# Latent attention: rotary partner by shifted products on VectorE, two banks for the first projections, and a part of the output projection in the last steps

## The reference

```python
def _mla(x, w_in, g_q, g_kv, w_uq, w_uk, w_uv, w_o, pos):
    h = x @ w_in                                   # 1024 -> 384 + 256 + 64
    c_q = _rmsnorm(h[..., :384], g_q)
    c_kv = _rmsnorm(h[..., 384:640], g_kv)
    k_r = _rope(h[..., 640:], pos)                 # one 64-wide rotary key for all heads
    q = einsum('bsr,rhd->bshd', c_q, w_uq)         # 8 heads of 128 + 64
    q_n, q_r = q[..., :128], _rope(q[..., 128:], pos)
    # scores: q_n . (w_uk c_kv) + q_r . k_r, scaled, causal; softmax; values w_uv c_kv
    return o @ w_o                                 # 1024 -> 1024
def _rope(x, pos):                                 # half = 32
    x1, x2 = x[..., :half], x[..., half:]
    return concatenate([x1 * cos - x2 * sin, x1 * sin + x2 * cos], -1)
```

## Time and profile before

| | |
|---|---|
| median of 3 runs | 2545.45 us (2542.76 to 2547.97) |
| the profiled execution's own time | 2543.65 us |
| its span | 2541.9 us |
| busy: PE, DVE, ACT, POOL | 2452.6, 1114.9, 886.0, 114.6 us |
| mean granted TensorE clock | 0.99 |
| matmuls | 11784 |

### The profile page before, as it was taken

The page is one execution under the profiler, slowest core; times in us unless marked ns, Lnnn a source line. Parts: engine busy times, 40 slices in busy tenths (PEclk is TensorE's granted clock), DMA queues, the critical chain, the costliest instruction groups (busy, mean ns, idle before and its releaser), DMA issues.

```text
span 2541.9 us, 29499 instructions
## 1 busy us (share of the span) xinstructions
PE 2452.6 (96%) x11784; PEld 2024.5 (80%) x11784; DVE 1114.9 (44%) x1487; ACT 886.0 (35%) x1444; POOL 114.6 (5%) x169
## 2 busy tenths in 40 slices
PE   7798999999989999998999999999999999999997
PEld 7577888888878788887888888888877788888886
DVE  3355633445665543346455322223245524433334
ACT  3232422323443332235444323332245534522222
POOL 3000200000100100000000000000000000000001
PEclk9999999999999999999999999999999999999999
DMA  5512332222311323322222222222321122322221
GB/s 161 75 54 67 117 100 100 90 92 83 108 42 50 118 98 100 99 100 67 78 71 81 92 92 83 83 83 84 104 67 50 51 94 80 108 99 91 96 94 67
DMA packets 187063, 220.32 MB, mean 87 GB/s; under 512 B 20531, under 2 KB 141568, under 8 KB 186832
## 3 DMA queue, kind: packets, MB, share of 16 engines
q1 hardware_dynamic: 183200, 206.13, 25.4%
q0 software_dynamic: 3760, 12.73, 2.4%
HBM read 213.60 MB, written 5.24 MB: 86 GB/s over the span
## 4 chain that ended last, share of the span: by engine, by line
PE 89%; DVE 6%; ACT 3%; issue 1%; DMA 1%; POOL 0%; SPq 0%; ACTq 0%; POOLq 0%; DVEq 0%
PE A L507 46%; PE B L507 40%; DVE WL L1754 2%; PE C L507 1%; ACT WH L1186 1%; DMA X<-in_x 1%; DVE Y L1912 1%; PE C L876 0%; PE C L1091 0%; DVE YL L1969 0%; DVE st L1893 0%; PE C L932 0%; ACT ar L1262 0%; DVE ar L1967 0%; ACT XH L1189 0%
## 5 line engine op out<-in xcount | busy, mean ns | idle before, releaser
L1754 DVE TENSOR_TENSOR WL<-RAW,WH 128x2048 fp32r<-128x2048 f32 (+1 forms) x197 | 448.8, 2278 | 690.1 <-ACT WH L1186 690.1
L1186 ACT ACTIVATE WH<-RAW 128x2048 fp32r<-128x2048 f32 (+1 forms) x197 | 370.9, 1883 | 626.0 <-PE A L507 561.1
L507 PE MATMUL B<-XH,WH 128*128 128x512 f32 (+1 forms) x1440 | 548.2, 385 | 8.7 <-DVE WL L1754 5.4
L507 PE MATMUL B<-XH,WL 128*128 128x512 f32 (+1 forms) x1440 | 539.9, 379 | 0.0
L507 PE MATMUL B<-XL,WH 128*128 128x512 f32 (+1 forms) x1440 | 526.5, 381 | 6.4 <-DVE XL L1769 6.3
L507 PE MATMUL A<-WH,YH 128*128 128x512 f32 x944 | 367.7, 390 | 1.6 <-DVE YL L2243 1.6
L507 PE MATMUL A<-WH,YL 128*128 128x512 f32 x944 | 367.3, 389 | 0.0
L507 PE MATMUL A<-WL,YH 128*128 128x512 f32 x944 | 367.2, 389 | 0.0
L507 PEld LDWEIGHTS B<-XH,WH 128*128 128x128 f32 x1440 | 271.8, 189 | 78.2 <-issue 16.4
L507 PEld LDWEIGHTS B<-XH,WL 128*128 128x128 f32 x1440 | 272.0, 189 | 51.3
L507 PEld LDWEIGHTS B<-XL,WH 128*128 128x128 f32 x1440 | 263.7, 190 | 57.1 <-DVE XL L1769 8.3
(11 more groups left out here) (290 smaller groups left out, 2125.9 us busy)
## 6 DMA issues: line engine op xcount, KB each, us to landing
RAW<-in_w_in SPq DMA_DIRECT2D x33, 1024.0 KB, 5.1
RAW<-in_mlp_w_up SPq DMA_DIRECT2D x32, 1024.0 KB, 5.2
RAW<-in_mlp_w_down SPq DMA_DIRECT2D x32, 1024.0 KB, 5.0
RAW<-in_w_in SPq DMA_DIRECT2D x48, 512.0 KB, 4.3
RAW<-in_w_ffn_in SPq DMA_DIRECT2D x22, 1024.0 KB, 5.1
RAW<-in_w_ffn_out SPq DMA_DIRECT2D x10, 1024.0 KB, 5.0
RAW<-in_mla_w_o SPq DMA_DIRECT2D x4, 1024.0 KB, 5.1
RAW<-in_swa_w_q SPq DMA_DIRECT2D x4, 1024.0 KB, 4.9
```

What stands on the lines that cost most here:

```text
L507: return nc.tensor.matmul(dst, l, r, start=first, stop=last)
L1186: nc.scalar.activation(WH[s][:, 0:n], RAW[s][:, 0:n], ACT.Copy).then_inc(hi_ready, 1)
L1754: tt(WL[s][:, 0:n], RAW[s][:, 0:n], f32(WH[s][:, 0:n]), ALU.subtract).then_inc(lo_ready, 1)
```

## The change

It makes these edits. Rotary partner: the second version of the rotary key and unit 5 of every pair are gone, with their loads; VectorE makes the sine product by four multiplications of 32 rows each, which read the bank 32 rows away (`rotated`). A pair has seven units now (0, 1 queries, 2 rotary queries, 3, 4 keys, 5, 6 values), its chunk 1664 columns. Stage "in": the rope matmuls of each half stand ahead of that half's keys, the queries are transposed between the halves, and the keys after two units of pair 0. The first eleven units alternate between B[0] and B[1]. The splits of chunks 8 and 10 come earlier in steps 1 and 5. Four groups of the output projection (first chunk, first 512 columns) run in steps 11 to 14 in B[0], and VectorE adds them to alpha x. GpSimd's constants wait for x, its first two gain vectors come after the roots, and its bias additions wait for one more chunk of the MLP. The split of chunk "if + 1", the low halves of the third norm, and the whole end of the feed-forward have new places: its last half runs block by block, gains are multiplied ahead of the root, ScalarE makes the root, and stores go by halves.

```diff
-    ("in", 4, 2, 2, 7, 1, 0),
+    ("in", 4, 2, 0, 7, 1, 0),
+    def unit_bank(n):
+        return n % 2 if n < PAIR_AHEAD else 0
+    def unit_taken(n):
+        if n < PAIR_AHEAD:
+            return s_("pair_u%d" % (n % 2)), n // 2 + 1
+        return s_("pair_u0"), (PAIR_AHEAD + 1) // 2 + n - PAIR_AHEAD + 1
+    def units_of(j):
+        i = (j + 6) // T
+        return i, () if i >= PAIRS else ((4,), (5, 6), (0, 1), (2, 3))[j % T]
-    PAIRS, PAIR_STEPS, PAIR_UNITS = 4, 16, 8
+    PAIRS, PAIR_STEPS, PAIR_UNITS, PAIR_AHEAD = 4, 16, 7, 11
@@ SP, end
+            for h in range(2):
+                cols = slice(512 * h, 512 * h + 512)
+                sp.wait_ge(s_("fin_x"), 2 * t + h + 1)
+                sp.dma_start(out[0, tok(t), cols], X[:, t, cols]).then_inc(s_("stored"), 16)
@@ TensorE
+        in_rope(0)
...
+        in_keys(0)
+        in_rope(1).then_inc(s_("in_rope"), 1)
+        queries_by_feature()
+        in_keys(1)
...
+            if n >= PAIR_AHEAD:
+                pe.wait_ge(*unit_taken(n - 1))
+            elif n >= 2:
+                pe.wait_ge(*unit_taken(n - 2))
+            elif n == 1:
+                pe.wait_ge(s_("rope_taken"), 1)
...
+        def output_part(t):
+            if t == 0:
+                pe.wait_ge(lo_ready, c + 1)
+                pe.wait_ge(*unit_taken(PAIRS * PAIR_UNITS - 1))
+                pe.wait_ge(s_("pair_lo"), 8)
+            else:
+                pe.wait_ge(s_("wo_x"), t)
+            for k in range(4):
+                r = mm3(B[0][:], XH[:, k, tok(t)], XL[:, k, tok(t)], wh[:, k, :], wl[:, k, :], k == 0, k == 3)
+        pair_unit(0, 0)
+        pair_unit(0, 1)
+        keys_by_feature()
+        for u in range(2, PAIR_UNITS):
             pair_unit(0, u)
...
-            i, u = (j + 6) // T, 2 * ((j + 2) % T)
-            if i < PAIRS:
-                pair_unit(i, u)
+            i, us = units_of(j)
+            for u in us[:1]:
+                pair_unit(i, u)
+            if 10 < j < 15:
+                output_part(j - 11)
             pair_values(j)
-            if i < PAIRS:
-                pair_unit(i, u + 1)
+            for u in us[1:]:
+                pair_unit(i, u)
...
-        tokens_half(BASE["wo0"][0], 0, BASE["wo0"][1], XH, XL)
+        tokens(BASE["wo0"][0] + 1, slot(BASE["wo0"][0] + 1), XH, XL, 4, 4, 512, BASE["wo0"][1])
...
+        for t, kh in ((0, 0), (1, 0), (0, 1), (1, 1), (2, 0), (2, 1), (3, 0), (3, 1)):
+            nk = (4, 2)[kh]
@@ ScalarE
+            if j in (1, 5):
+                split(c0 + 4 + j // 2, more=16 * 2 + 192 + 64 * (j // T))
             if j + 2 < PAIR_STEPS:
                 pair_exp(j + 2)
...
+        split(BASE["if"][0] + 1)
         then_root("pre", 3)
...
+                if h:
+                    act.wait_ge(s_("fin_ss"), T + t + 1)
+                    act.wait_ge(s_("fin_half"), t + 1)
+                    nc.scalar.activation(stat(RS + t), stat(SS + 4 + t), ACT.Sqrt, bias=stat(SS + t)).then_inc(s_("fin_root"), 1)
@@ VectorE
+        def rotated(bank, scale=None):
+            half = ROPE // 2
+            for q in range(4):
+                to, of = slice(half * q, half * q + half), slice(half * (q ^ 1), half * (q ^ 1) + half)
+                if scale:
+                    x = stt(M_T[to, 1, :], bank[of, :], scale, sinT[to, :], ALU.mult, ALU.mult)
+                else:
+                    x = tt(M_T[to, 1, :], bank[of, :], sinT[to, :], ALU.mult)
+            return x
...
+                then(rotated(bank))
+                x = tt(M_T[:, 0, :], bank[:], cosT, ALU.mult)
...
+            x = X[:, t, 0:512]
+            stt(x, x, ALPHA, B[0][:], ALU.mult, ALU.add).then_inc(s_("wo_x"), 1)
...
+            if t == 3:
+                lo_half("post", 0, range(4), NG2, ALU.mult)
             product_out(1, t)
...
+        def first_half(t):
+            dve.wait_ge(s_("fin_ss"), t + 1)
+            then(tt(Y[:, t, 0:512], Y[:, t, 0:512], GB[:, 0, 0:512], ALU.mult))
+            ts(stat(SS + t), stat(SS + t), RMS_EPS, None, ALU.add).then_inc(s_("fin_half"), 1)
+        def add_normed(t):
+            dve.wait_ge(a_free[t], ra + 6)
+            then(tt(xtmp[:, t % 2, :], Y[:, t, 512:1024], GB[:, 0, 512:1024], ALU.mult))
+            dve.wait_ge(s_("fin_root"), t + 1)
+            then(nc.vector.reciprocal(stat(RS + t), stat(RS + t)))
+            for h, y in enumerate((Y[:, t, 0:512], xtmp[:, t % 2, :])):
+                x = X[:, t, 512 * h:512 * h + 512]
+                stt(x, y, stat(RS + t), x, ALU.mult, ALU.add).then_inc(s_("fin_x"), 1)
...
+                    elif n == 2 and h == 0:
+                        if t == 3:
+                            split(c + 3)
+                        else:
+                            first_half(t - 1)
@@ GpSimd
+        pool.wait_ge(x_in[T - 1], 16)
...
-        pool.wait_ge(chunk_done, BASE["mlp0"][0] + 1)
+        pool.wait_ge(chunk_done, BASE["mlp0"][0] + 2)
```

More of the change, by code:

```diff
@@ L676, in _ @@
                             k == 0, k == 7)
[L677 to L683, removed]
+                if t == T - 1:
                     r.then_inc(chunk_done, 1)
@@ L686, in _, with queries_by_feature @@
                     r.then_inc(s_("in_kv"), 1)
+        def queries_by_feature():
+            for k in range(3):
+                u = n0 + 2 + k
+                pe.wait_ge(c_free[u % 2], u // 2)
+                for t in range(T):
+                    pe.wait_ge(a_free[t], ra + 1)
+                    r = nc.tensor.transpose(C[u % 2][:, tok(t)], C_N[:, t, tok(k)], ident[:])
+                r.then_inc(s_("in_t"), 1)
+        in_rope(0)
         pe.wait_ge(rows_in, ROWS_N * 16)
@@ L703, in _, with keys_by_feature @@
+        queries_by_feature()
+        in_keys(1)
         pe.wait_ge(masks_done, 1)
         pe.wait_ge(consts_done, 1)
+        in_c = n0
+        def keys_by_feature():
+            for k in (3, 4):
+                u = in_c + 2 + k
+                pe.wait_ge(c_free[u % 2], u // 2)
+                for t in range(T):
+                    pe.wait_ge(a_free[t], BASE["in"][1] + 2)
+                    r = nc.tensor.transpose(C[u % 2][:, tok(t)], C_N[:, t, tok(k)], ident[:])
+                r.then_inc(s_("in_t"), 1)
@@ L1162, in _ @@
             c, use, done = c + tiles, use + tiles, done + tiles
-            for h in range(2):
+            for h in range(2 if n < 2 else 1):
                 for kh in range(2):
@@ L1215, in _ @@
         split(1)
-        split(2, more=16 * 6)
+        split(2, more=16 * 2)
         act.wait_ge(s_("st_zero"), 1)
@@ L1276, in _ @@
         split(c0 + 1)
-        pair_unit(0, 2)
-        pair_unit(0, 6)
-        split(c0 + 2, more=16 * 6 + 256)
+        latents_hi((3, 4))
+        pair_unit(0, 3)
+        pair_unit(0, 5)
+        split(c0 + 2, more=16 * 2 + 128)
         pair_exp(0)
@@ L1878, in _ @@
             pair_weights(j)
+            if j in (1, 5):
+                split(c0 + 4 + j // 2)
             if j + 2 < PAIR_STEPS:
                 pair_max(j + 2)
-            if i < PAIRS and u == 4:
-                pair_unit(i, u)
-            pair_lo(j)
-            if i < PAIRS:
-                pair_unit(i, u + 1)
-            if j in (1, 5):
-                split(c0 + 4 + j // 2)
-            elif j in (2, 6, 9, 10):
+            for u in us[:1]:
+                if u in (2, 4):
+                    pair_unit(i, u)
+            if 10 < j < 15:
+                output_part(j - 11)
+            pair_lo(j)
+            for u in us[1:]:
+                if u in (1, 6):
+                    pair_unit(i, u)
+            if j in (2, 6, 9, 10):
                 split(c0 + (5 + (j // T) * 2 if j < 9 else j - 1))
@@ L2348, in _ @@
             for h in range(2):
-                split(c + 1)
-                split(c + 2)
+                if n < 2 or h == 0:
+                    split(c + 1)
+                    split(c + 2)
                 for t in range(T):
@@ L2480, in _ @@
         load_gb(a["norm_gains_2"][0, 1])
-        def root_of_halves(name, wait, t):
-            wait(t)
-            then(tt(stat(SS + t), stat(SS + t), stat(SS + 4 + t), ALU.add))
-            over_root(RS + t, SS + t, RMS_EPS, s_(name + "_r"))
         pool.wait_ge(s_("post_x"), T)
         load_gb(a["norm_gains_2"][0, 3])
-        for t in range(T):
-            root_of_halves("fin", lambda t: pool.wait_ge(s_("fin_ss"), T + t + 1), t)
     ctx.close()
```

259 lines of the change are left out of this document (146 added, 113 removed).

## The result

The changed kernel takes **2507.54 us** (median of 4 runs, 2501.42 to 2508.56) against 2544.11 (4 runs, 2542.66 to 2547.97) for the kernel before in the same set of runs: ratio 0.9849, 95% interval 0.9829 to 0.9869. The prediction was 2511, with a range of 2498 to 2524. It is the slowest of its four, and the medians differ by 36.6.

What follows compares the result with a forecast made beforehand. TensorE was taken as the bound, busy 2452.6 of 2541.9 us, idling mostly in the attention stages. The terms summed to -34.3 us from 2543.65, giving 2509.4, and with 1.8 for the median 2511 us, range 2498 to 2524.

Steps and rivals of the forecast that it cites:

- Start: Before the first projection: constants and gain vectors moved behind x let it land earlier, -4.3 us (bounds 0 and 4.3).
- First projections and pair 0 to step 0: Up to step 0's first weight transposes: fewer matmuls, two banks, but a held load of pair 1's values; -12.9 us.
- rival B: Load of chunk 7 not held by the table's transfer: step 0 starts at 88, -10 us, 2501; chance 0.15.
- Rival A: The table's transfer holds the load of chunk 7 to its end: +8 us, 2519; chance 0.19.
- Clock and steps 0 to 9: TensorE's clock after the wait before step 0, +2.0 us; steps 0 to 9, partner products gone, rope's bank busy longer, -5.3.
- I take 0.61: Rope in steps 0 to 9: us per 32-row shifted product from start to start, between bounds of 0.53 and 0.69.
- Output part: Four groups of the output projection moved into steps 11 to 14 fill TensorE's idle time: -2.7 us (bounds 0 and 4).
- Bias addition: Both MLPs: GpSimd's addition a chunk later cuts two TensorE waits of 2.2 us to 0.3 left; -3.8 us.
- Gates stage: Next chunk's split goes into a 4.4 us wait on VectorE, so TensorE's 2.09 wait at 1192.98 goes: -2.1 us.
- Tail: After the last matmul 6.4 us instead of 14.3, less a new wait of 2.7 for the last chunk's split: -5.2 us.
- C: Edits outside attention pay half: MLP wait moves with the addition, late last split eats the tail; +6, 2517; chance 0.09.
- D: Five ropes' 20 shifted products run slow; from 2.0 us more apiece beyond 0.61 the whole gain is gone; chance 0.05.

Runs made afterwards that it cites:

- e3: The changed kernel without GpSimd's wait for x, so its constants go out at once again, gain vectors still behind the roots: 2515.35 us, ratio 0.9902.
- e1: The changed kernel with the 3 MB table of biases written only when chunks 8 and 9 have landed: 2497.16 us, ratio 0.9822.
- e13: The changed kernel with each shifted product of 32 rows and 512 columns cut into two of 256 columns: 2507.35 us, ratio 0.9853.
- e4: The changed kernel with the four groups of the output projection back behind the steps: 2511.76 us, ratio 0.9881.
- e5: The changed kernel with GpSimd's bias addition in both MLPs one chunk earlier again: 2512.7 us, ratio 0.9873.

## Why the prediction came out

*Start.* Right: the constants took DMA time from x. 5.5 in the ledger and 5.0 in e3 against 4.3 forecast; against the middle start of 13.9 they are 4.6 and 4.1.

*First projections and pair 0 to step 0.* -13.0 against -12.9, and for the reason given; that it fits to 0.1 is luck. Counted as in the prediction (5.5 added), the first product of pair 0 starts at 56.3 instead of 58.1 and the load is issued at 61.9 instead of 63.9, but it is held longer: 26.9 us to landing instead of 25. It was issued at 56.4 and landed at 83.3 (forecast near 60 and near 85), without a packet at first (the first goes at 70 to 71) and then one packet for one. That is what the earlier trace rows had shown for the kernel before; e1 priced it at 8.3 where the prediction said 8 (96 against 88). The Trainium skill's rule (DMA: Bandwidth & Descriptors, Queues, rings and completion order: each engine goes round the queues that have work) describes the second half, 174 and 171 packets; it does not describe 60 to 68, when the load moved nothing, and rival B, built like it, had step 0 some 8 us too early. Rival A fell too: the load landed before the table did.

*Clock and steps 0 to 9.* -2.8 against -3.3, but the two terms were each off. The rope's waits were 1.83 and 1.82, not 1.5, and that of the fifth product 2.25, not 1.9: 0.35 more each, which is four products at 0.70 instead of the 0.61 that the prediction took from start to start. So the step that was mis-sized is "I take 0.61". The rule that the prediction set against it (the Trainium skill, VectorE: DVE Perf Modes, Two Vector instructions with no wait between them: an operation whose input or output starts in another group of 32 partitions than that of the last one is held until the earlier ones are done) agrees with e13's 0.34 and 0.42. The clock was charged with 2.0, for the wait before step 0 alone. Steps 0 to 9 ran at 0.95, which is 3.5 to 4 us of 78.7, about half of it behind that wait and half behind the one at 151.6; the fall in the last steps stood in the kernel before too.

*Output part.* -3.8 in the ledger and 4.1 in e4 against -2.7. The idle time that it fills was sized right, 2.8. The rest stands in TensorE's busy time (21.9 + 10.9 without the part, 31.6 with it), and what makes it smaller these runs do not tell.

*Bias addition.* -3.8 forecast, 5.0 measured by e5 for what the addition does, against 4.4 for the two waits of 2.2. 0.3 per MLP was kept for a rest that did not appear; the remainder to the ledger's 6.7 is clock.

*Sliding-window attention.* The missing term: +4.1, of which 3.5 lie in the three stretches with the lower granted clock, in a stage that the change does not touch. The second profile of the changed kernel has the same clocks there, 0.71, 0.60 and 0.66. Gains by clock elsewhere (first MLP 1.7, start of the diff stage 1.6) nearly cancel it, and that is luck, not forecast.

*Gates stage.* -1.8 against -2.1, the right size by another way than the prediction said. The 2.09 at 1192.98 is gone, but 11 us later, where the kernel before did not wait (its transposes at 1205.72 follow at once), TensorE waits 2.11 for the chain of the gates (1176.17, above). So no idle time was saved. VectorE's part of that chain comes 1.8 earlier, and TensorE with it; the prediction left out that the chain, and not the split, comes last. The table by stretch over this turn, from the first matmul of the same product on, first before, then after:

```profile
1192.98:1220.00 27.02, 27.02 (x115) 22.08 (x116) 16.27 (x21) 13.79 (x15) 0.00 (x0) 0.94 0.33 107
```

```profile
1162.97:1190.45 27.48, 25.37 (x117) 20.84 (x116) 16.53 (x21) 13.80 (x15) 0.00 (x0) 1.00 0.25 77
```

The same work takes 27.0 us without an idle moment at 0.94, and 27.5 with the new wait at 1.00: what the clock gives back, some 1.6 us, goes into that wait. *Third norm:* -0.3 against 0.

*Tail.* -3.8 against -5.2. The new wait was foreseen (2.33 against 2.7). The end was not: 7.9 us after the last matmul instead of 6.4. The prediction priced the last block alone and took VectorE as free when it comes. In the timeline the blocks are one chain of 3.39 us each: copy, product with the gains, 0.46 for the root, inverse, two halves.

*Rivals C and D.* C fell in its first half: no wait moved with the addition. Its second half, that the late split eats into the tail, stood in the forecast too and came at 2.33 us. D fell: 0.70 a product, far from the 2.0 above 0.61 from which it would have decided (1.7 by its own count, 34.3 us over 20 products).

## What to carry to other kernels

A small load issued just behind a big transfer of another queue can wait out a large part of it; hold the big one back until the small ones that somebody waits for have landed, and a second bank is then worth twice as much (8.2 against 3.8 us at the first step). Order VectorE's queue by who waits: one normalising moved ahead of work that nobody needed yet brought the first step 3.6 us forward, nearly as much as two removed partner products (2.0 each). And do not read a few microseconds off one stage without its granted clock beside it.

## What the hardware showed unexpectedly

A 256 KB load took 26.9 us with a 3 MB transfer of the other queue started 3 us before it, and 2.6 without. Two VectorE operations of 256 columns that read PSUM overlap by 0.08 us (0.42 long, 0.34 apart) unless the group of 32 rows changes, then not at all. The granted clock of one and the same untouched stage was 0.71 to 0.82 in one kernel and 0.60 to 0.71 in the other, at a cost of 3.5 us in 30; both profiles of the changed kernel agree in it, and the versions of the experiments lie between. What decides it was not settled by these runs.
